# Six modulation rows summed as quarters on four groups of output rows, and spread by DMAs from ScalarE's queue

## What is computed

```python
m = jax.nn.silu(cond) @ w_mod + b_mod        # w_mod 1024 x 6144 per layer
sh1, sc1, g1, sh2, sc2, g2 = jnp.split(m, N_MOD, axis=-1)
hx = modulate(x, sh1, sc1)                   # h * (1 + scale) + shift
...                                          # attention (layer 0) or pooling (layer 1) gives y_lat
x = layer_norm(ALPHA * x + g1 * y_lat, ln_g[i, 0], ln_b[i, 0])
x = layer_norm(ALPHA * x + g2 * swiglu(modulate(x, sh2, sc2), ffn_w_in[i], ffn_w_out[i]), ...)
```

## Time and profile before

| | |
|---|---|
| runs of the kernel, us | 1129.48, 1129.6, 1132.5; median 1129.6 |
| profiled execution: its own time, us | 1130.3 |
| profiled execution: span, us | 1128.4 |
| PE busy | 1116.9 us, 99% |
| DVE busy | 766.8 us, 68% |
| ACT busy | 574.2 us, 51% |
| POOL busy | 62.5 us, 6% |
| DMA moved | 236.77 MB, mean 210 GB/s |

### The profile page before, as it was taken

How to read it: one execution, slowest core, us unless ns; L and a number is a source line. 1 busy time by engine, 2 the same in 40 slices (tenths; PEclk the granted TensorE clock), 3 DMA queues, 4 the chain that set the end, 5 groups by cost and what they waited for, 6 DMA issues and landing times.

```text
span 1128.4 us, 15464 instructions
## 1 busy us (share of the span) xinstructions
PE 1116.9 (99%) x6357; PEld 946.9 (84%) x6357; DVE 766.8 (68%) x898; ACT 574.2 (51%) x801; POOL 62.5 (6%) x121
## 2 busy tenths in 40 slices
PE   8999999999999999999999999999999999999998
PEld 4688767889998887999988878877888889998886
DVE  2497588889799797975554865455657667664454
ACT  3542367554444436544443767464765365553342
POOL 0011130002111101000000000000000000000000
PEclk9999999999999999999999999999999999999999
DMA  9986750769998865885555797785634446555541
GB/s 328 379 290 229 256 169 8 254 238 331 352 343 298 323 221 181 269 268 161 186 189 148 164 239 169 164 169 129 173 112 149 150 157 237 180 179 202 203 158 38
DMA packets 120567, 236.77 MB, mean 210 GB/s; under 512 B 5665, under 2 KB 61282, under 8 KB 120370
## 3 DMA queue, kind: packets, MB, share of 16 engines
q1 hardware_dynamic: 105984, 184.89, 53.0%
q0 software_dynamic: 14224, 50.64, 13.0%
q10 hardware_dynamic: 290, 0.26, 0.1%
HBM read 234.72 MB, written 1.05 MB: 209 GB/s over the span
## 4 chain that ended last, share of the span: by engine, by line
PE 87%; DVE 3%; ACT 1%; DMA 1%; issue 0%; ACTq 0%; DVEq 0%
PE ps L2015 18%; PE ps L2017 17%; PE ps L2016 17%; PE ps L2057 8%; PE ps L2058 8%; PE ps L2056 8%; PE ps L2162 2%; PE ps L2339 1%; PE ps L2301 1%; DMA raw<-in_ffn_w_out 1%; PE ps L2212 1%; DVE wL L1172 1%; PE ps L2587 0%; PE ps L2538 0%; PE ps L2544 0%
## 5 line engine op out<-in xcount | busy, mean ns | idle before, releaser
L1172 DVE TENSOR_TENSOR wL<-raw,wH 128x1024 fp32r<-128x1024 f32 x326 | 394.9, 1222 | 232.0 <-ACT wH L644 230.8
L644 ACT ACTIVATE wH<-raw 128x1024 fp32r<-128x1024 f32 x326 | 340.1, 1058 | 361.5 <-PE ps L2017 212.8
L2015 PE MATMUL ps<-wH,aH 128*128 128x512 f32 x576 | 229.0, 398 | 1.1 <-DVE aL L1606 0.4
L2016 PE MATMUL ps<-wL,aH 128*128 128x512 f32 (+1 forms) x592 | 228.8, 387 | 0.0
L2017 PE MATMUL ps<-wH,aL 128*128 128x512 f32 x576 | 224.7, 390 | 0.0
L2056 PE MATMUL ps<-aH,wH 128*128 128x256 f32 x768 | 219.4, 286 | 0.0
L2058 PE MATMUL ps<-aH,wL 128*128 128x256 f32 x768 | 217.3, 283 | 0.0
L2057 PE MATMUL ps<-aL,wH 128*128 128x256 f32 x768 | 217.3, 283 | 0.0
L2057 PEld LDWEIGHTS ps<-aL,wH 128*128 128x128 f32 x768 | 147.4, 192 | 1.0 <-issue 1.0
L2056 PEld LDWEIGHTS ps<-aH,wH 128*128 128x128 f32 x768 | 147.4, 192 | 1.0 <-DVE wL L1172 0.7
L2058 PEld LDWEIGHTS ps<-aH,wL 128*128 128x128 f32 x768 | 147.4, 192 | 0.0
(11 more groups left out here) (349 smaller groups left out, 1288.8 us busy)
## 6 DMA issues: line engine op xcount, KB each, us to landing
raw<-in_ffn_w_in SPq DMA_DIRECT2D x88, 512.0 KB
modraw<-in_w_mod POOLq DMA_DIRECT2D x80, 512.0 KB, 6.3
raw<-in_w_in SPq DMA_DIRECT2D x32, 1024.0 KB
raw<-in_ffn_w_out SPq DMA_DIRECT2D x22, 1024.0 KB
raw<-in_w_up SPq DMA_DIRECT2D x16, 1024.0 KB
raw<-in_w_down SPq DMA_DIRECT2D x16, 1024.0 KB
mod<-in_w_mod SPq DMA_DIRECT2D x8, 1024.0 KB, 11.8
raw<-in_attn_w_qkv SPq DMA_DIRECT2D x8, 1024.0 KB
```

Of the source, the lines that this page charges most:

```text
L644: nc.scalar.activation(wHigh(n), raw[:, (n // 2) % RAW, (n % 2) * 1024:(n % 2) * 1024 + 1024], ACT.Copy).then_inc(w_hi, 1)
L1172: V.tensor_tensor(wL[:, n % WL, :], raw[:, (n // 2) % RAW, (n % 2) * 1024:(n % 2) * 1024 + 1024], wHigh(n).bitcast(fp32), ALU.subtract).th ...
L2015: T.matmul(outp, xh, h, start=first, stop=False, skip_group_check=part_of)
L2016: T.matmul(outp, xh, l, start=False, stop=False, skip_group_check=part_of)
```

## The change

For the six row vectors PE no longer makes the sum on all 128 partitions. `vec_total` issues four matmuls of 32 columns of ones by 256 columns of the tile. Quarter j of the vector goes to output rows 32j to 32j+31, all four in the same 256 columns of bank 6 (bank 0 for v = 0). `vec_put` is one DVE instruction of 128x256 with the bias quarters, which lie in one half of `modrow` (`quarters(v)`, halves in turn), loaded by four DMAs of 32x256 (`load_bias`). Then `row_out(v)` on ACT's queue waits for that put and issues 16 DMAs of 32x256 (32 KB each) from `modrow` to the destination: quarter j to each of the four groups of partitions. For the second to fifth of the six it also issues the four DMAs of the next vector's bias, once the spreading before has landed. Those who read the rows wait for the landing (`row_ready`). The bias loads of 128x1024 are gone from SP's and POOL's queues; POOL loads the quarters of the first two.

```diff
+ROW_VECS = (0, 3, 4, 5, 6, 9)
...
+        def quarters(v):
+
+            i = (ROW_VECS.index(v) + 1) % 2
+            return modrow[:, 256 * i:256 * i + 256]
+
+        def load_bias(eng, v, done):
+
+            layer, m = VECS[v]
+            for j in range(4):
+                c0 = m * D + 256 * j
+                eng.dma_start(quarters(v)[32 * j:32 * j + 32, :],
+                              a["b_mod"][layer:layer + 1, c0:c0 + 256].to_broadcast([32, 256])).then_inc(done, 16)
...
-                if layer == 0:
-                    sp.wait_ge(o_out, 4)
-                    for dst, j in ((sh1b, 0), (sc1b, 1)):
-                        sp.dma_start(dst[:, :], a["b_mod"][1:2, j * D:(j + 1) * D].to_broadcast([P, D]))\
-                            .then_inc(bias1_in, 16)
...
+            def row_out(v):
+
+                i = ROW_VECS.index(v)
+                dst = {0: g1b, 3: g2b0, 4: sh1b, 5: sc1b, 6: g1b, 9: g2b1}[v]
+                act.wait_ge(mod_out, NMOD0 + v + 1)
+                for j in range(4):
+                    for q in range(4):
+                        act.dma_start(dst[32 * q:32 * q + 32, 256 * j:256 * j + 256], quarters(v)[32 * j:32 * j + 32, :])\
+                            .then_inc(rows_out, 16)
+                if 1 <= i < len(ROW_VECS) - 1:
+                    act.wait_ge(rows_out, 256 * i)
+                    load_bias(act, ROW_VECS[i + 1], bias2_in)
...
+                if c == 3:
+                    row_out(0)
...
+                    if layer == 0 and c in FF0_PUT:
+                        row_out(FF0_PUT[c])
+                    elif (layer, c) == (1, 8):
+                        row_out(IN_FF0)
...
+                    if layer == 0 and k == 6:
+                        row_out(6)
...
-                    V.scalar_tensor_tensor(out=dst2, in0=ps[:, b:b + 2, :], scalar=one, in1=dst2,
+                    V.scalar_tensor_tensor(out=quarters(v), in0=ps[:, 0 if v == 0 else 6, 0:256], scalar=one, in1=quarters(v),
                                            op0=ALU.add, op1=ALU.add).then_inc(mod_out, 1)
...
-                    for b in range(2):
-                        ins = T.matmul(ps[:, (6 if v else 0) + b, :], cst[:, C_ONE:C_ONE + P], row[:, b * CW:(b + 1) * CW],
-                                       start=True, stop=True)
+                    for j in range(4):
+                        ins = T.matmul(ps[32 * j:32 * j + 32, 6 if v else 0, 0:256], cst[:, C_ONE:C_ONE + 32],
+                                       row[:, 256 * j:256 * j + 256], start=True, stop=True)
```

More of the change, by code:

```diff
@@ L371, in build @@
         vec_step, vec_sum = sem("vec_step"), sem("vec_sum")
-        bias0_in, bias1_in, gbias_in, pscale_in = (sem(n) for n in ("bias0_in", "bias1_in", "gbias_in", "pscale_in"))
+        bias_in, bias2_in, rows_out, pscale_in = (sem(n) for n in ("bias_in", "bias2_in", "rows_out", "pscale_in"))
         rows_T, cT_zero, cT_ready = sem("rows_T"), sem("cT_zero"), sem("cT_ready")
@@ L562, in _ @@
                 .then_inc(small_in, 16)
-            pool.dma_start(g1b[:, :], a["b_mod"][0:1, 2 * D:3 * D].to_broadcast([P, D])).then_inc(bias0_in, 16)
+            pool.wait_ge(mod_out, NMOD0)
+            load_bias(pool, ROW_VECS[0], bias_in)
             for v in range(1, IN_QKV):
@@ L566, in _ @@
             pool.wait_ge(vec_step, KT * IN_QKV)
-            pool.dma_start(g2b0[:, :], a["b_mod"][0:1, 5 * D:6 * D].to_broadcast([P, D])).then_inc(bias0_in, 16)
             for j, nm in enumerate(("norm_mix_2", "norm_mlp_2", "norm_ple_2")):
@@ L593, in _ @@
             pool.wait_ge(acc_out, UNITS["wo"] + 2)
-            pool.dma_start(g1b[:, :], a["b_mod"][1:2, 2 * D:3 * D].to_broadcast([P, D])).then_inc(gbias_in, 16)
+            load_bias(pool, ROW_VECS[1], bias_in)
             vec_load(IN_QKV + 1)
@@ L604, in _ @@
             pool.wait_ge(t_done, GROUPS["pool"] + 4)
-            pool.wait_ge(mod_out, NMOD0 + IN_FF0)
-            pool.dma_start(g2b1[:, :], a["b_mod"][1:2, 5 * D:6 * D].to_broadcast([P, D])).then_inc(gbias_in, 16)
             vec_load(IN_FF0)
@@ L1275, in vec_put, with row_ready @@
                 else:
[L1276 to L1282, removed]
-                    else:
-                        dve.wait_ge(bias1_in, 32)
-                    dst2 = dst[:, :].rearrange("p (b c) -> p b c", b=2)
-                    b = 0 if v == 0 else 6
-                    V.scalar_tensor_tensor(out=dst2, in0=ps[:, b:b + 2, :], scalar=one, in1=dst2,
+                    i = ROW_VECS.index(v)
+                    if i < 2:
+                        dve.wait_ge(bias_in, 64 * (i + 1))
+                    else:
+                        dve.wait_ge(bias2_in, 64 * (i - 1))
+                    V.scalar_tensor_tensor(out=quarters(v), in0=ps[:, 0 if v == 0 else 6, 0:256], scalar=one, in1=quarters(v),
                                            op0=ALU.add, op1=ALU.add).then_inc(mod_out, 1)
+            def row_ready(v):
+                dve.wait_ge(rows_out, 256 * (ROW_VECS.index(v) + 1))
             V.memset(g1b[:, 0:CW + P], 0.0).then_inc(zeros, 1)
@@ L1481, in ln @@
                         lo_t(name, 0, norm=norm)
+                    if t == 0:
+                        row_ready(0 if k == 0 else IN_FF0)
                     product_done(stage, t)
@@ L1610, in ln_pool @@
                 dve.wait_ge(ln_x, TT)
+                row_ready(3)
                 residual(0)
@@ L1686, in beside @@
                             dve.wait_ge(ln_in, 64)
-                            dve.wait_ge(mod_out, NMOD0 + 6)
+                            row_ready(5)
                             link(V.tensor_tensor(tfrow, lnp[:, 1, :], sc1b[:, :], ALU.mult))
@@ L1738, in swiglu @@
                             dve.wait_ge(pscale_in, 16)
+                            row_ready(6)
                             link(V.tensor_tensor(g1b[:, :], g1b[:, :], psb[:, :], ALU.mult))
```

## The result

The changed kernel takes 1152.34 us (median of four runs, 1149.23 to 1153.41), the kernel before 1130.97 beside it: ratio 1.0183, 95% interval 1.0161 to 1.0205. It is 21 us slower, where 4 us faster was forecast. The profiled execution has a span of 1151.3 us, 22.9 more than before. Where single executions fall far outside the others (one of experiment 6 took 4247.91 us), the ratios leave them out.

The account below looks back on a forecast made before the run. PE, busy for 99% of the span, was taken to bound the kernel; 3.1 us at pooling plus 0.94 at v = 9 made 4.0, so 1129.6 - 4.0 = 1125.6 us. Range 1123.2 to 1131.2, the forecast's own 1125.0 to 1127.0.

Parts of the forecast that it names:

- PE's saving: At each of the six totals PE would take 0.77 us instead of 1.71, saving 0.94 each, 5.6 us in all.
- DVE's saving: Each put would take 0.42 us instead of 1.22, saving 0.8, which by itself gives nothing where PE leads.
- What ACT takes on: Each DMA issue on ACT would take 0.33 us (bounds 0.28 and 1.26), so 20 issues of a row_out 6.6 us.
- v = 5: At this total in in0 PE would come at 312.42 and wait 0.8 us for DVE's last product.
- v = 7 and the landing: PE would wait 0.2 us at v = 7; out0's weight load would land at 385.3; pooling would move by 3.1 us.
- the rival's formula: At an issue of i us, DVE is ready to restart before pooling at 385.1 + 40 (i - 0.33).
- The term for the landing itself: Sharing queues with the spreading adds 0.6 us (bounds 0 and 1.7) to the landing of out0's weight load.
- The clock: In pooling the lower granted clock behind PE's wait costs some 1.7 us once; once more would leave 2.3 of the 4.0.
- ACT holds DVE too long, slower: Longer ACT issues delay DVE past the landing from 0.40 us each; 1131.5 us at 0.51; chance 0.19, half slower by over 0.3%.
- Quarters don't overlap: At the six totals the four quarters run without overlap, 0.34 us more each, with ACT's load 1132 to 1134; chance 0.06.
- All arrives: Issues cost ACT next to nothing, PE never waits for vec_steps, all 5.6 us arrive: 1124.0 us; chance 0.17.
- part is lost on the way: Pooling gains only 0 to 2 us, through issues of 0.36 to 0.45 or lost clock: 1127.3 us; chance 0.20.

Follow-up runs that it names:

- experiment 6: Changed kernel with the spreadings of v = 3 to 6 cut up, four of the 20 issues behind each of five successive weight copies on ACT: ratio 1.0067 to the kernel before.
- 3: Changed kernel with each spreading DMA of 32x256 split into two of 32x128, 32 issues instead of 16: ratio 1.0723 to the kernel before.
- 5: Changed kernel with groups of four DMAs of several kinds added on three queues; on ACT's queue issues 0.64 us apart SBUF to SBUF, 0.47 with one end in HBM.
- experiment 1: Changed kernel with the spreading through HBM from ACT's queue, 3 issues per row instead of 20: ratio 0.9977 to the kernel before, 0.9981 in a second set.
- experiment 2: Changed kernel with one 128x1024 DMA of the bias row from HBM in place of the 16 spreading DMAs, 5 issues instead of 20: ratio 0.9967 to the kernel before.
- 4: Kernel before, totals and puts kept, with ACT issuing 16 DMAs of 32x256 at four places and four bias DMAs more at three: ratio 1.0198 to the kernel before.
- 7: Changed kernel with the spreadings of v = 3, 4 and 5 behind the copy into hH instead of ahead of it: ratio 1.018 to the kernel before.
- 8: Changed kernel with only v = 4 spread by 16 DMAs, the others by one DMA of the bias row from HBM: ratio 1.005 to the kernel before.
- 9: Changed kernel with only v = 6 spread by 16 DMAs, the others by one DMA of the bias row from HBM: ratio 1.002 to the kernel before.
- 10: Changed kernel with the same 16 + 4 DMAs per row issued from POOL's queue instead of ACT's: ratio 1.0104 to the kernel before.

## Why the prediction was wrong, step by step

**PE's saving: right.** 0.76 us per total, foretold 0.77; 0.95 saved, foretold 0.94. **DVE's saving: right** in size: the put takes 0.41.

**What ACT takes on: wrong, and this is the step that failed.** An issue was sized at 0.33 us, "since these are ACT's own rows". It is 0.64 for the 16 from SBUF to SBUF and 0.50 to 0.53 for the four of the bias; a `row_out` is 12.4 to 13.4 us instead of 6.6. The rows were loads from HBM, and none goes from SBUF to SBUF. That explains 0.47 against 0.64. It does not explain 0.33 against 0.47, both with one end in HBM: why the issues at the start of the kernel are cheaper stays open. The same timeline had one row more, ACT's first issue, which the prediction left out:

```profile
0.81 0.61 ACTq L699 DMA_DIRECT2D rows<-in_c  x1
```

So ACT's own rows did not stop at 0.36. The argument against a high price, fewer descriptors, was beside the point: rows and columns do not matter (experiments 3 and 5). The bound of 1.26 held the value. The Trainium skill (DMA: Bandwidth & Descriptors, Anatomy of one DMA) gives about 50 ns for the sequencer's part, told there for GpSimd's path. The distance between issues is far above it on every queue here; POOL's are 0.50 apart.

**v = 5: right place, wrong size.** The wait is 8.0 instead of 0.8. PE comes at 312.57, foretold 312.42. By the prediction's own slope, 0.2 per 0.01 us, 0.31 more gives 0.8 + 6.2 = 7.0, which comes near; the block also took 0.5 more than 20 x 0.64, and it began at 303.16 instead of 302.55, as the put of v = 4 ended only at 303.12 (302.71 + 0.41), foretold 301.8. DVE behind `row_out(4)` and `(5)` is idle 6.45 and 11.29 us with ACT as releaser, as named.

**v = 7 and the landing: wrong place.** `row_out(5)` was said to cost 0.2 us at v = 7, DVE's saved puts taking the hold back. PE was stopped earlier, 8.9 us at the start of out0, a point that the prediction did not look at: the reserve there was 0.35 us, less than at the two totals that it weighed (1.9 and 3.2). This wait and the clock are why the rival's formula is too small as well: with i = 0.64 it gives 397.5 - 389.5 = 8.0 us at DVE's restart, less 0.9, 1137 us in all. (By that formula 3.4 us are reached at i = 0.55, not 0.56.) The term for the landing itself was sound: 0.6 foretold, with bounds of 0 and 1.7, and where the issues are few it is 0.7 and 1.6 (experiment 1 and its repetition, counted as what the load takes longer from issue to landing).

**The clock: seen, too small.** It was one loss of 1.7 in pooling. Four stretches at half the clock cost an estimated 8.8 us more than before.

**The rivals.** "ACT holds DVE too long, slower" came true in mechanism; its price was capped by the belief in the earlier trace rows. "Quarters don't overlap" is refuted. "All arrives", 5.6 us, did not come even with few issues: experiment 1 gains 2.1 to 2.6 and experiment 2 some 3.7. The way through HBM, with medians of 1127.75 and 1127.6, is near "part is lost on the way", 1127.3, and for one of its reasons: pooling gains only 1.2 and 1.5. The range ended at 1131.2 and should have reached, by the bound of 1.26 that stood in the text, far beyond.

Shown: the issues on ACT are the cause (1, 2, 3, 4 agree from four sides, and 6 keeps every DMA and takes away over half of the loss), and each hold stops DVE's list (7, 8, 9). That traffic of the small DMAs is harmless is shown only up to PE's arrival at the total of v = 5 (10). How much of the 8.8 us of clock a given wait causes was read from windows, not tried.

## What to carry to other kernels

Cost a DMA issue by a row of the same kind (both ends in SBUF or one in HBM) and count it as work of the engine whose queue issues it: twenty issues held ScalarE's queue for 13 us, as long as a dozen weight copies, and with it every consumer behind them in program order. Few wide transfers through HBM (one out, one broadcast back) did the same spreading with 3 issues and made the change 0.2% faster than before instead of 1.8% slower. Before counting a gain on an engine that leads, find the smallest reserve of the next engine over the whole stretch, bank by bank, not only at the instructions that the change touches.

## What was not expected of the hardware

- The issue of a DMA from SBUF to SBUF takes 0.64 us on ACT's queue, whether it is 1x256, 32x16, 32x256 or 128x64, and on SP's (32x256); on ACT's with one end in HBM it takes 0.47, but 0.32 to 0.36 when it is the first of a group, and 0.32 to 0.35 for the single broadcast to 128x1024 in experiment 1. The 4x256 from SBUF to HBM there takes 0.50 to 0.59, each alone, too, so the ends and the place in a group are not all that sets the price. On POOL's queue both kinds take 0.50.
- While PE waited for 8.0 us its granted clock fell to 0.50 at 316.5, 4 us before it resumed, and stayed there for 6.1 us of work after it. The short wait of 2.57 us is followed by 3.3 us of work at 0.50.
